# Mixture-of-experts decoder layer: an expert's two up pieces loaded as one 8 MB transfer, token chunks by every eighth column

## The reference

```
logits = (xt @ w_router + b_router)
top_val, top_idx = lax.top_k(logits, TOP_K)              # TOP_K = 4 of N_EXPERTS = 32
combine = softmax(top_val) scattered to (tokens, experts)
for e in range(N_EXPERTS):
    hid = clamped_swiglu(xt @ w_mlp1[e] + b_mlp1[e])     # w_mlp1[e]: 1024 x 2048, 8 MB
    y = y + combine[:, e:e + 1] * (hid @ w_mlp2[e] + b_mlp2[e])   # w_mlp2[e]: 1024 x 1024, 4 MB
```

## Time and profile before

| | us |
|---|---|
| median of 3 runs | 1142.33 |
| the runs | 1141.17, 1142.33, 2108.56 |
| span of the profiled execution | 1139.4 |
| TensorE busy | 1088.4 (96% of the span) |
| DVE busy | 320.1 |
| ACT busy | 224.3 |
| bytes read from HBM | 445.21 MB, 392 GB/s over the span |

### The profile page before, as it was taken

How to read it: one execution, slowest core, us unless ns; L and a number is a source line. 1 busy time by engine, 2 the same in 40 slices (tenths; PEclk the granted TensorE clock), 3 DMA queues, 4 the chain that set the end, 5 groups by cost and what they waited for, 6 DMA issues and landing times.

```text
span 1139.4 us, 15654 instructions
## 1 busy us (share of the span) xinstructions
PE 1088.4 (96%) x6516; PEld 522.4 (46%) x6517; DVE 320.1 (28%) x723; ACT 224.3 (20%) x403; POOL 9.1 (1%) x14
## 2 busy tenths in 40 slices
PE   7999999999999999999999999999999999999996
PEld 6888899844333333334333333333333333334321
DVE  6887775562111111111211111111111101012113
ACT  5566565431000001001100000000000001001001
POOL 0000000000000000000000000000000000000000
PEclk9999999989999999999999999999999999999999
DMA  9766867599999999999999999999999999999995
GB/s 358 275 201 229 280 226 259 229 404 430 433 438 426 439 428 437 431 434 436 429 438 428 438 427 439 427 439 429 436 433 433 436 429 437 427 430 430 429 428 247
DMA packets 39967, 446.72 MB, mean 392 GB/s; under 512 B 4480, under 2 KB 5120, under 8 KB 24096
## 3 DMA queue, kind: packets, MB, share of 16 engines
q1 hardware_dynamic: 39936, 446.27, 93.6%
HBM read 445.21 MB, written 1.05 MB: 392 GB/s over the span
## 4 chain that ended last, share of the span: by engine, by line
PE 60%; DMA 36%; DVE 2%; SPq 1%; ACT 1%; issue 0%; DVEq 0%
DMA ring<-in_w_mlp 36%; PE bank L1025 24%; PE bank L1063 9%; PE bank L619 5%; PE bank L621 5%; PE bank L620 5%; PE bank L947 4%; PE bank L935 2%; PE bank L984 1%; PE bank L839 1%; PE bank L823 1%; PE bank L999 1%; SPq L452 1%; DMA live<-in_x_cols 0%; PE bank L606 0%
## 5 line engine op out<-in xcount | busy, mean ns | idle before, releaser
L1025 PE MATMUL bank<-ring,live 128*64 128x512 f32 x2048 | 472.9, 610 | 25.6 <-DMA ring<-in_w_mlp 25.0
L1025 PEld LDWEIGHTS bank<-ring,live 128*64 128x64 f32 x2048 | 144.7, 139 | 311.9 <-issue 293.2
L1063 PE MATMUL bank<-ring,live 128*64 128x512 f32 x992 | 220.3, 596 | 4.3 <-DMA ring<-in_w_mlp 4.3
L1743 DVE COPY live<-bank 128x256 f32<-128x256 f32 x32 | 13.6, 425 | 525.6 <-PE bank L977 525.6
L1063 PEld LDWEIGHTS bank<-ring,live 128*64 128x64 f32 x992 | 68.2, 137 | 130.1 <-issue 121.8
L1357 ACT ACTIVATE live<-bank 128x512 f32<-128x512 f32 x31 | 18.5, 597 | 324.4 <-PE bank L984 324.4
L1827 DVE TENSOR_SCALAR live<-bank 128x256 f32<-128x256 f32 x64 | 24.2, 420 | 198.9 <-PE bank L1025 198.9
L1429 DVE TENSOR_TENSOR w_low<-w_raw,w_high 128x1024 fp32r<-128x1024 f32 x63 | 74.5, 1221 | 15.4 <-ACT w_high L1152 14.9
L619 PE MATMUL bank<-w_high,left 128*128 128x512 f32 x160 | 64.4, 402 | 7.2 <-DVE w_low L1599 7.1
L1152 ACT ACTIVATE w_high<-w_raw 128x1024 fp32r<-128x1024 f32 x63 | 64.7, 1063 | 27.9 <-DMA w_raw<-in_w_in 12.7
L1353 ACT ACTIVATE live<-live 128x512 f32<-128x512 f32 x32 | 20.3, 635 | 246.1 <-DVE live L1827 246.1
(11 more groups left out here) (224 smaller groups left out, 788.3 us busy)
## 6 DMA issues: line engine op xcount, KB each, us to landing
ring<-in_w_mlp SPq DMA_DIRECT2D x73, 4096.0 KB, 46.9
ring<-in_w_mlp SPq DMA_DIRECT2D x42, 2048.0 KB, 48.3
w_raw<-in_w_in SPq DMA_DIRECT2D x23, 512.0 KB, 8.8
w_raw<-in_w_mem_kv SPq DMA_DIRECT2D x16, 512.0 KB, 5.0
ring<-in_w_mlp SPq DMA_DIRECT2D x8, 1024.0 KB, 37.5
w_raw<-in_w_mix_out SPq DMA_DIRECT2D x8, 512.0 KB, 5.6
w_raw<-in_w_mem_q SPq DMA_DIRECT2D x8, 512.0 KB, 3.8
w_raw<-in_w_mem_o SPq DMA_DIRECT2D x8, 512.0 KB, 5.1
```

Of the source, the lines that this page charges most:

```text
L1025: mm = pe.matmul(up[j][64 * g:64 * g + SLOTS, :], x_e[:, k, :], columns(row, j, g), start=False, stop=(k == KC - 1))
L1063: mm = pe.matmul(to[64 * g:64 * g + SLOTS, :], stationary[:, P * c + 64 * u:P * c + 64 * u + SLOTS], slot(at)[:, col:col + 512], start=(u ...
```

## The change

The up weights of an expert are laid out over the partitions anew: partition p holds rows 8p to 8p+7 of the matrix, which is one run of 64 KB in HBM. For e4 to e27 both up slots of a parity are filled by one transfer of 8 MB, issued when TensorE has finished the up stage of expert e-2 (`up_done`), and it counts up `piece_in` of the first slot alone. TensorE waits for that before chunk 0 and no longer before chunk 4. The halves of e0 to e3 and e28 to e31 stay transfers of 2 MB with 16 KB in a run per partition, cut from the new layout. Token chunk c is now every eighth column, starting at c.

```diff
+        def all_up(e):
+
+            return a["w_mlp1"][0, ds(e, 1), :, :].rearrange("a (p c) n -> p (a c n)", c=8)
+
         def expert_src(e, k):
 
             if k < UPS:
-                rows = a["w_mlp1"][0, ds(e, 1), 4 * P * k:4 * P * (k + 1), :]
-                return rows.rearrange("a (p c) n -> p (a c n)", c=4)
+                return all_up(e)[:, 8192 * k:8192 * (k + 1)]
...
             def load_up(e, before, parity):
 
-                for k in range(UPS):
-                    if k:
-                        sp.wait_ge(up_done, before + 1)
-                    else:
-                        sp.wait_ge(up_used, before * 3 + 2)
-                    load(e, k, 3 * parity + k)
+                sp.wait_ge(up_done, before + 1)
+                sp.dma_start(ring[:, NHALF * parity:NHALF * parity + 8, :].rearrange("p a n -> p (a n)"), all_up(e))\
+                    .then_inc(piece_in[3 * parity], 16)
...
                 for i in range(2):
                     for q in range(2):
-                        at = 512 * q + S * i
-                        mm = pe.matmul(banks[3 + 4 * i][64 * q:64 * q + SLOTS, 0:S], pick_first[:, t, :], h2[:, t, at:at + S],
+                        cols = h2[:, t, :].rearrange("p (m c) -> p m c", c=KC)[:, 64 * i:64 * (i + 1), 4 * q:4 * (q + 1)]
+                        mm = pe.matmul(banks[3 + 4 * i][64 * q:64 * q + SLOTS, 0:S], pick_first[:, t, :], cols,
...
                         t, part = n // 3, n % 3
-                        at = 4 * P * (c // 4) + c % 4
-                        mm = pe.matmul(xg[:, SLOTS * c:SLOTS * (c + 1)], h_parts[:, t, part, at:at + 4 * P - 3:4],
+                        mm = pe.matmul(xg[:, SLOTS * c:SLOTS * (c + 1)], h_parts[:, t, part, c:KC * P:KC],
                                        pick[:, t, :], start=(n == 0), stop=(n == 5))
...
-                    if k % 4 == (2 if first_loads else 0):
-                        pe.wait_ge(piece_in[at + k // 4], loads)
+                    if k == (2 if first_loads else 0):
+                        pe.wait_ge(piece_in[at], loads)
+                    if first_loads and k == 6:
+                        pe.wait_ge(piece_in[at + 1], first_loads)
```

## The result

| | us |
|---|---|
| before, beside it | 1142.40 |
| changed, median of 4 runs | 1158.93 (1158.42 to 1159.03) |
| ratio | 1.0151, 95% interval 1.0139 to 1.0163 |
| span of the profiled execution | 1156.3 (before 1139.4) |

The change makes the kernel 1.5% slower, 16.5 us by the medians and 17.3 by the ratio. That is within the 2% for which "same" stood, but outside the range (1142 to 1157). The ratio is taken over fast runs alone, so without the run of 2108.56 us of the kernel before. In the two traces the last scatter starts at 1128.24 before and at 1145.11 after, 16.9 us later, and what follows it is as long (11.2 us).

The account below looks back on a forecast made before the run. TensorE bounds first, then the DMA queue. Queue gap +5.5 and rate -1.9 give +3.6 from loads; TensorE's tail ends later at +4.9, with the clock +5.8: 1148.1 us, range 1142 to 1157.

Parts of the forecast that it names:

- e27: Expert 27, the last with a merged up load: forecast to land at 990.8 instead of 987.2 us.
- same: Whole kernel: time within 2% (22.8 us) of the kernel before, chance 0.91; faster 0.01, slower 0.08.
- What bounds, and the two regimes: Expert stages: first TensorE sets the pace (26.0 us an expert), then the DMA queue (29.0 us, 434 GB/s).
- the strides: Gather's stationary slice, 8 to 16 bytes between columns: taken as 0, upper end 70 ns a pair.
- Rival A: Gather slows by D us an expert, 7D in all; 18 ns a pair gives 1154, 70 ns 1207; chance 0.17.
- The queue at the first big load: First 8 MB up loads, near 300 us: late issue runs the queue dry twice, +5.5 us at the later.
- I take 2.6: First 8 MB load on an empty queue: 2.6 us from issue to landing beyond its transfer; alternative 1.4.
- The rate: Up loads in the middle: larger merged runs move 0.4% faster, -1.9 us, nothing at the least.
- TensorE behind the landing: From the last merged load's landing to the last scatter: TensorE needs 142.3 us, last scatter 4.9 us later.
- The clock: Waits of 3.0 us drop the clock at every second expert; at e27 +1.7 or nothing, middle taken.
- B: Larger runs fetched slower or faster: 1% slower 1153, 1% faster 1145, 2% passed at 3.7% slower; chance 0.09.
- C: The 64 KB run is moved as two of 32 KB, so the saving is gone: 1150; chance 0.10.

Follow-up runs that it names:

- experiment 8: Kernel before with the gather's stationary slices cut at steps of 1 to 16 bfloat16 columns (wrong tokens, same work); ran once, 1143.5 us.
- experiment 2: Changed kernel with up weights in two 4 MB pieces with the issues and waits of before; new layout and slow gather kept: 1144.23 us, ratio 1.0020.
- experiment 1: Kernel before with both up pieces in one 8 MB transfer behind `up_done`, old layout and gather (32 KB runs): 1150.53 us, ratio 1.0077.
- experiment 3: Changed kernel with the stride undone: tokens' parts in groups of four, gather of every fourth column: 1150.94 us, ratio 1.0078.
- experiment 5: Kernel before, stride undone, two 4 MB pieces both issued behind `up_done`, TensorE waiting for each at its own chunk: 1147.84 us, ratio 1.0051.
- experiment 6: Changed kernel with stride undone and two pieces with the issues of before, TensorE waiting for both ahead of chunk 0: 1143.05 us, ratio 1.0017.
- experiment 4: Changed kernel with the first four merged experts' up weights back in two pieces with the issues of before, gather still slow: 1153.53 us, ratio 1.0109.
- experiment 7: Changed kernel with stride undone and the first four and last two merged experts' up weights back in 4 MB pieces: 1142.75 us, ratio 1.0005.

## Why the prediction was wrong

**What bounds, and the two regimes: right.** The waits in the middle, the loads' rate of 434 GB/s and the full DMA share stayed.

**The step that failed: the strides, "I take 0".** The gather was the term that I had bounded from 0 to 70 ns a pair and put at the lower end, because the float32 transposes with 16 bytes between columns kept their pace of 148 ns. It measured 27 ns a pair (62.5 - 35.6), 1.30 us an expert. The reading that misled is the row of L984: its load is 70 ns longer, but its transposes start 148 ns apart, and experiment 8 puts 128 new lines at 62 ns. That fits into 148 ns and not into the 36 ns at which the bfloat16 pairs follow each other. This is worked out; no run changed the stride of the float32 transposes. The weight load that grew (212 against 142) was the row to believe. Rival A had the mechanism and the multiplier right: 7 x 1.30 = 9.1 us, and 5.8 + 9.1 = 14.9, so 1157.2 where 1158.9 was measured. Undoing the stride brought back 8.

The multiplier is the part to keep. Alone, the slow gather costs 2.3 us (experiment 2), and the merged transfer alone 8.8 (experiment 1); together they cost 16.5 and not 11.1. The traces show where the gather costs more. With the merged transfer (changed kernel against experiment 3) it makes up e27 land 4.5 us later, since the load goes out at `up_done`, and it adds 3.4 us to TensorE's way from there to the last scatter. With separate pieces (experiment 2 against the kernel before) the landing is 2.9 us later and nothing is added behind it (141.1 us against 141.0), because the loads still end last there.

**The queue at the first big load: right in mechanism, short in size.** The queue ran dry twice near 300 us, and the late issue alone cost 5.8 us. Mis-sized was the time from issue on an empty queue, "I take 2.6": it measured 3.8 and 3.7 (23.2 and 23.1 less 19.4), and 4.3 for up e5, which was even issued 1.6 us before the queue emptied. It isn't a fixed time ahead of each load: in experiment 5 a first piece of 4 MB landed 2.3 us after its bytes' own time, and the rest of the 3.7 came with the piece behind it. The shift at up e5 is 11.1 us: 5.5 forecast, 3 x 1.30 = 3.9 from the gather, 1.7 from this.

**The rate: mis-sized by half.** The merged transfers with 64 KB runs brought 1.0 us from e5 to e27 (638.0 us between their landings instead of 639.0), where I had 1.9. With 32 KB runs (experiment 1) they brought 0.3.

**TensorE behind the landing: right.** From TensorE's start on e27 to the last scatter it is 142.3 us on record, 142.5 in experiment 6; with the slower gather 142.3 + 4 x 1.30 = 147.5, measured 147.6 from 997.47. The clock: the alternation is there (experiment 6), but in the changed kernel it doesn't occur, since the slower gather leaves waits of 1.3 to 1.5 us. The 0.9 that I had for it falls away, while in experiments 1 and 3 a fall at e27 did cost its 1.7.

The sum of the changed kernel, by its own trace: 11.1 - 1.0 + (147.8 - 141.0) = 16.9 us at the last scatter, which is what it shows. From the forecast's +5.8 it is 9.1 for the gather, 1.7 for the time to landing and 0.9 for the rate, less 0.9 for the clock: 16.6.

**Two sums among the rivals don't come out.** B's 1153 for loads 1% slower keeps the saving of 1.9 that it takes away; without it 1155, and 2% is passed at 3.3% slower. A at 18 ns with C is 1156 and not 1157. Neither bears on the step that failed.

**Open.** In experiment 4 a piece that was issued 6.3 us before the queue emptied (304.55 against a landing at 310.9) still landed 1.5 us late, and in experiment 7 the first merged transfer, issued 6.0 us ahead (411.36 against a landing at 417.4), 1.2 us late. In experiment 2 the second piece of e4 was 1.5 us late with 6.9 us in hand. In the kernel before, the same piece with 7.8 us in hand landed on time, the first piece of e4 did with 6.0, and in the changed kernel the 8 MB of e6 did with 6.1. How far ahead an issue must be is not settled by these runs. That the loss moves with the time of issue is shown (experiment 5).

## What to carry to other kernels

Merging two transfers moves the earlier one's issue to the later one's release. Where a queue is at its shortest, count what it still holds at that moment, and allow nearly 4 us (measured here for 8 MB) from issue to landing beyond the bytes. Then every delay on the engine that gives the release counts again in the queue.

A layout that makes a DMA's runs longer makes someone else's stride longer. Look at the stationary operands first: keep a bfloat16 slice at three columns of step or fewer where pairs follow each other as closely as here, or store it in the order in which it is read. A slower step that hides in idle time today stops hiding when the slack moves.

## What the hardware showed that I had not expected

A weight load of 128 bfloat16 columns that opens a new 16-byte line per column goes with a pace of 62 to 63 ns a pair, at two and three columns of step 31 to 32 ns. The float32 loads with the same 16 bytes between columns are longer too (212 against 142 ns), while the transposes keep their pace (148 against 155 ns).

8 MB on an empty queue landed 3.7 to 3.8 us after their bytes' own time (23.1 and 23.2 us less 19.4), as one transfer or as two pieces; 3.8 us for 512 KB leave 2.6. Issuing 1.0 to 1.6 us ahead of the end of the queue still left 2.7 us between the landings beyond the bytes.
